# A fifth pair of units with seven block products in each layer, behind one plain unit whose down projection stands on both sides of the pair's first block

## The reference

```python
FFN_HIDDEN = 5632

def swiglu(h, w_gate, w_up, w_down):
    return (jax.nn.silu(h @ w_gate) * (h @ w_up)) @ w_down

for layer in range(2):
    h = rms_norm(x, mix_norm[layer])
    mix = ...                      # mixer of the layer
    x = x + mix
    h = rms_norm(x, ffn_norm[layer])
    x = x + swiglu(h, w_gate[layer], w_up[layer], w_down[layer])
return rms_norm(x, final_norm)
```

## Time and profile before

| | |
|---|---|
| time, median of 3 runs | 1944.07 us (1942.9 to 1945.13) |
| the profiled execution | 1944.98 us, span 1943.2 us |
| granted TensorE clock, mean | 0.997 |
| TensorE busy | 1925.4 us, 99% |
| VectorE busy | 1395.8 us, 72% |
| ScalarE busy | 924.5 us, 48% |
| DMA | 380.92 MB, mean 196 GB/s |

### The profile page before, as it was taken

The page is one execution under the profiler, slowest core; times in us unless marked ns, Lnnn a source line. Parts: engine busy times, 40 slices in busy tenths (PEclk is TensorE's granted clock), DMA queues, the critical chain, the costliest instruction groups (busy, mean ns, idle before and its releaser), DMA issues.

```text
span 1943.2 us, 21963 instructions
## 1 busy us (share of the span) xinstructions
PE 1925.4 (99%) x9268; PEld 1612.3 (83%) x9268; DVE 1395.8 (72%) x1040; ACT 924.5 (48%) x722; POOL 23.6 (1%) x85
## 2 busy tenths in 40 slices
PE   9999999999999999999999999999999999999997
PEld 7889999988888888888888887788888888888885
DVE  5656788865758868877779556756877868878754
ACT  6434434436434535545446345633544545545443
POOL 1000000000000000000000030000000000000000
PEclk9999999999999999999999999999999999999999
DMA  9555444455555654846666655464675654747751
GB/s 305 177 176 166 152 152 151 151 176 171 178 191 198 235 195 173 281 153 250 226 215 229 214 187 173 132 208 137 236 261 190 243 195 174 278 139 252 240 211 70
DMA packets 214730, 380.92 MB, mean 196 GB/s; under 512 B 5921, under 2 KB 55154, under 8 KB 214386
## 3 DMA queue, kind: packets, MB, share of 16 engines
q1 hardware_dynamic: 214560, 379.62, 57.5%
q10 hardware_dynamic: 82, 0.03, 0.0%
HBM read 377.53 MB, written 2.10 MB: 195 GB/s over the span
## 4 chain that ended last, share of the span: by engine, by line
PE 90%; DVE 8%; ACT 1%; issue 1%; DVEq 0%; POOL 0%; ACTq 0%; POOLq 0%
PE main L1576 39%; PE main L1582 20%; PE main L1518 8%; PE aux L1598 5%; PE main L1520 4%; DVE lo L976 4%; DVE raw L982 4%; PE aux L1602 3%; PE main L1598 2%; PE aux L1525 2%; PE main L1602 2%; PE aux L1687 1%; ACT hi L628 1%; PE main L1629 1%; PE main L1631 1%; PE main L1630 1%
## 5 line engine op out<-in xcount | busy, mean ns | idle before, releaser
L628 ACT CAST hi<-raw 128x2048 fp32r<-128x2048 f32 (+1 forms) x389 | 741.6, 1907 | 779.1 <-PE main L1582 494.1
L976 DVE TENSOR_TENSOR lo<-raw,hi 128x2048 fp32r<-128x2048 f32 x316 | 720.0, 2291 | 321.6 <-ACT hi L628 321.6
L1576 PE MATMUL main<-hi,act 128*128 128x512 f32 x1968 | 470.0, 391 | 0.0
L1576 PEld LDWEIGHTS main<-hi,act 128*128 128x128 f32 x1968 | 368.1, 188 | 77.5 <-issue 1.9
L1576 PE MATMUL main<-hi,mid 128*128 128x512 f32 x1664 | 397.0, 391 | 0.3 <-DVE mid L1243 0.3
L1576 PEld LDWEIGHTS main<-hi,mid 128*128 128x128 f32 x1664 | 310.8, 188 | 65.3 <-DVE mid L1243 1.0
L1582 PE MATMUL main<-lo,act 128*128 128x512 f32 x984 | 243.1, 389 | 0.0
L1518 PE MATMUL main<-act,hi 128*128 128x512 f32 x640 | 229.1, 401 | 0.0
L967 DVE TENSOR_TENSOR lo<-raw,hi 128x2048 fp32r<-128x2048 f32 x71 | 162.6, 2290 | 79.2 <-ACT hi L628 79.2
L1582 PEld LDWEIGHTS main<-lo,act 128*128 128x128 f32 x984 | 184.7, 188 | 38.3
L1582 PE MATMUL main<-lo,mid 128*128 128x512 f32 x832 | 205.5, 389 | 0.0
(11 more groups left out here) (169 smaller groups left out, 1287.9 us busy)
## 6 DMA issues: line engine op xcount, KB each, us to landing
raw<-in_ffn_w_gate SPq DMA_DIRECT2D x104, 1024.0 KB, 5.2
raw<-in_ffn_w_up SPq DMA_DIRECT2D x88, 1024.0 KB, 6.3
raw<-in_ffn_w_down SPq DMA_DIRECT2D x88, 1024.0 KB, 5.1
raw<-in_ab_w_in SPq DMA_DIRECT2D x55, 1024.0 KB, 5.1
raw<-in_ab_w_out SPq DMA_DIRECT2D x16, 1024.0 KB, 5.1
raw<-in_pool_w SPq DMA_DIRECT2D x4, 1024.0 KB, 5.5
xn<-in_x SPq DMA_DIRECT2D x4, 512.0 KB, 7.9
out<-xn SPq DMA_DIRECT2D x2, 768.0 KB, 4.2
```

The lines of the kernel that those rows point to most:

```text
L628: return nc.scalar.copy(out_, in_)
L976: V.tensor_tensor(lo[:, split_at(t), :], src, hi[:, split_at(t), :].bitcast(F32), ALU.subtract).then_inc(lo_ready, 1)
L1576: mm(o2[:, h, :], lhs[:, k0 + n, c, h * P:(h + 1) * P], w_hi, start=(first and c == 0 and n == 0), stop=False)
```

## The change

`UNITS` becomes `(3, 2, 2, 2, 2)`: the first group of a layer is one plain unit and a pair, the other four are pairs. Ten pairs in all. The class `Plain` goes, and `Group` has its pair's first unit as `a`.

The plain unit (unit 0) has 8 slots of gate and up as before. Its down projection no longer adds up with that of other units: it is four slots of its own, `early`. The order of the first group's slots is: gate and up of the plain unit (8), `ups[0]` of the pair (4, into `bank_a`; behind its second slot the hidden tile of the plain unit is turned), early 0 and 1, block 0 (6), early 2 and 3, block 1 (6), `g.x` (2), `ups[1]` (4), down of the pair (8). Early 0 goes into `bank_b`, early 1 into `bank_a`, and early 2 and 3 both into `bank_b`, one token half at a time (`early_half`), with two new semaphores: `half_used` (TensorE is done with half 0) and `half_added` (VectorE has added half 0 into `xn`). In the last group of a layer the three turnings of `xn` (layer 0) or the three products with the final gain (layer 1) stand behind down slots 4, 5 and 6 (`AFTER`).

```diff
-UNITS = (2, 2, 2, 2, 3)
+UNITS = (3, 2, 2, 2, 2)
...
+PAIR_DOWN = ((0, 0), (1, 0), (0, 1), (1, 1), (2, 0), (2, 1), (3, 0), (3, 1))
+AFTER = {4: 0, 5: 1, 6: 2}
...
+        g = Group(layer, u + n - 2, len(UNITS) * layer + index)
+        if g.first:
+            g.slot, g.job = s, j
+            up_a = s + 8
+            k0 = up_a + 4 + 2
+            k1 = k0 + BLOCK + 2
+            g.early = (up_a + 4, up_a + 5, k0 + BLOCK, k0 + BLOCK + 1)
+            j += 6
```

On VectorE (ScalarE has the same order of `prepare`, without `early_down`):

```diff
+                def up_a(g):
+
+                    for b in range(4):
+                        prepare(g.ups[0] + b + AHEAD)
+                        if g.first and b == 1:
+                            take_hidden(layer, g.a - 1, 0)
+
+                def early_down(g, m):
+
+                    xs = xn[:, :, WIDE * m:WIDE * (m + 1)]
+                    if m < 2:
+                        add_residual(Count(g.early[m]), (bank_b, bank_a)[m], m)
+                        return
+                    for h in range(2):
+                        if h == 0:
+                            ve.wait_ge(half_used, 2 * layer + m - 1)
+                        else:
+                            ve.wait_ge(slot_used, g.early[m] + 1)
+                        V.tensor_tensor(xs[:, h], xs[:, h], bank_b[:, h, :], ALU.add
+                                        ).then_inc(half_added if h == 0 else job_emptied, 1)
...
+                        up_a(g)
+                        for m in range(2):
+                            early_down(g, m)
+                            prepare(g.early[m] + AHEAD)
+                    for i in range(BLOCK):
+                        prepare(g.blocks[0] + i + AHEAD)
+                    if g.first:
+                        for m in range(2, 4):
+                            early_down(g, m)
+                            prepare(g.early[m] + AHEAD)
+                    else:
+                        up_a(g)
                     if g.blocks:
-                        for i in range(BLOCK):
-                            prepare(g.blocks[0] + i + AHEAD)
-                        for b in range(4):
-                            prepare(g.ups[0] + b + AHEAD)
                         for i in range(BLOCK):
                             prepare(g.blocks[1] + i + AHEAD)
```

On TensorE:

```diff
@@ gate_block @@
                 product(s + 2, bank_q3, sum_tiles(k, 1, 0), start, end)
+                if k == 0 and g.first:
+                    pe.wait_ge(job_emptied, g.job + 4)
                 product(s + 3, bank_q6, sum_tiles(k, 0, 0), start, end)
...
+                def up_a(g, bank_):
+
+                    for b in range(4):
+                        wide(g.ups[0] + b, bank_, act, 4 * b, b == 0, b == 3)
+                        if g.first and b == 1:
+                            pe.wait_ge(job_emptied, g.job + 2)
+                            turn_hidden(layer, g.a - 1, 1)
+
+                def early_half(s, m, h):
+
+                    if m == 3:
+                        pe.wait_ge(half_added if h == 0 else job_emptied, 2 * layer + 1 if h == 0 else g.job + 5)
+                    at = split_at(s)
+                    for n in range(4):
+                        w_hi, w_lo = (a[:, at, n * WIDE:(n + 1) * WIDE] for a in (hi, lo))
+                        t_hi, t_lo = (mid[:, n, c, h * P:(h + 1) * P] for c in range(2))
+                        mm(bank_b[:, h, :], t_hi, w_hi, start=(n == 0), stop=False)
+                        mm(bank_b[:, h, :], t_lo, w_hi, start=False, stop=False)
+                        ins = mm(bank_b[:, h, :], t_hi, w_lo, start=False, stop=(n == 3))
+                    ins.then_inc(half_used if h == 0 else slot_used, 1)
...
+                        pe.wait_ge(job_emptied, g.job + 1)
+                        up_a(g, bank_a)
+                        pe.wait_ge(turn_taken, T_HIDDEN[layer] + 1)
+                        wide(g.early[0], bank_b, mid, 0, True, True)
+                        pe.wait_ge(up_kept, g.pair + 1)
+                        wide(g.early[1], bank_a, mid, 0, True, True)
                     if g.blocks:
-                        pe.wait_ge(job_emptied, g.j_up - 1)
+                        pe.wait_ge(job_emptied, g.job + 3 if g.first else g.j_up - 1)
                         need(pe, gates_out, g.pair)
                         pe.wait_ge(a_ready, 2 * layer + 1)
                         gate_block(g, 0)
...
+                        if g.first:
+                            for m in (2, 3):
+                                s = g.early[m]
+                                pe.wait_ge(hi_ready, s + 1)
+                                pe.wait_ge(lo_ready, s + 1)
+                                early_half(s, m, 0)
+                                early_half(s, m, 1)
+                            pe.wait_ge(job_emptied, g.j_up - 1)
```

More of the change, by code:

```diff
@@ L88 @@
     layer: int
-    unit: int
-    n: int
-    pair: int = 0
+    a: int
+    pair: int
     blocks: tuple = ()
@@ L95 @@
     j_up: int = 0
-    plain: tuple = ()
+    slot: int = 0
+    job: int = 0
+    early: tuple = ()
     down: tuple = ()
@@ L122, in ffn_groups @@
     for index, n in enumerate(UNITS):
-        g = Group(layer, u, n, (len(UNITS) - 1) * layer + index - 1)
-        alone = range(n) if g.first else range(2, n)
-        if not g.first:
-            k0, up_a, k1 = s, s + BLOCK, s + BLOCK + 4
[L127 to L136, removed]
+        g = Group(layer, u + n - 2, len(UNITS) * layer + index)
[7 more added lines that the diff above has]
+        else:
+            k0, up_a, k1 = s, s + BLOCK, s + BLOCK + 4
+        g.blocks, g.x = (k0, k1), k1 + BLOCK
+        g.ups, g.j_up = (up_a, g.x + 2), j
+        s, j = g.x + 6, j + 1
+        g.down, g.j_down = tuple((s + k, m, i) for k, (m, i) in enumerate(PAIR_DOWN)), j
+        s, j, u = s + 8, j + 4, u + n
         out.append(g)
@@ L521, in gate_block @@
                 for p, (row, u) in zip(PLACES[g.blocks[k]], ((0, 0), (0, 1), (1, 1), (1, 0))):
-                    place(p, wide_rows(w_gate[layer], WIDE * (2 * k + row), WIDE * (g.unit + u)))
+                    place(p, wide_rows(w_gate[layer], WIDE * (2 * k + row), WIDE * (g.a + u)))
             def unit(w, s, u):
@@ L1408, in _ @@
                 for g in groups:
                     c21, e = sig[:, 1, :], g_of[:, 1, 1, :]
-                    u0 = 2 * (UNIT_ALL * layer + g.unit)
+                    u0 = 2 * (UNIT_ALL * layer + g.a)
+                    if g.first:
+                        for b in range(8):
+                            s = g.slot + b
+                            if b == 3:
+                                ve.wait_ge(row_rstd, norm + 1)
+                                gate_out(layer, g.a - 1, 1, norm, T_HIDDEN[layer])
+                            if b == 7:
+                                ve.wait_ge(job_emptied, g.job + 1)
+                                up_out(s, 1, norm)
+                            prepare(s + AHEAD)
+                            start_of_layer(layer, b, norm)
+                        up_a(g)
+                        for m in range(2):
+                            early_down(g, m)
+                            prepare(g.early[m] + AHEAD)
```

176 lines of the change are left out of this document (84 added, 92 removed).

## The result

The changed kernel takes 1955.38 us (median of 6 runs, 1953.91 to 1956.43), the kernel before 1943.78 beside it (6 runs, 1942.90 to 1945.13). The ratio is 1.0057, with a 95% interval of 1.0047 to 1.0068: 0.6% slower, where 1953.4 us was predicted.

A forecast was written before the change was run, and what follows sets the result against it. TensorE, busy 99% of the span, was taken to bound the kernel, so matmuls removed are time gained and waits time lost. -9.6 + 2 x 7.8 + 3.4 = +9.4 us on the median 1944.07 gave 1953.4; range 1946.5 to 1957.0.

The forecast's parts named there:

- Block 0: First pair's block 0: TensorE waits for early_down(0) and lo of products 2 and 3; 2.55 us of waits, +2.2 us.
- Early 3: Half 0 of early 3 waits for VectorE's half addition, queued behind block 1's first lo and two sums: +5.7 us a layer.
- the late and the punctual case: Load for block 1's first product: if late, early 3 waits 5.7 us; if punctual, 4.1.
- Rival (c): At half 0 of early 3, additions into xn do not hold TensorE up: 1934.5 us; chance 0.05 with its neighbours.
- The clock: Around early 3's wait the clock falls, eight to nine matmuls run at 0.427 us: 1.7 us a layer, +3.4 us.
- Block 1: First pair's block 1, behind early 3: no wait, as VectorE is ahead for once; -0.2 us a layer.
- The fifth pair and what costs nothing: Each layer's fifth pair replaces two plain units: -9.6 us for two layers; extra additions, splits, sums and turnings cost nothing.

The follow-up runs named there:

- the experiments on the order: Changed kernel with early 2's half additions on VectorE moved ahead of block 1's first preparation and between its lo and sums: 1944.82 us, ratio 1.0007 to the kernel before.
- VectorE's path: Changed kernel with one more same-size subtraction on VectorE ahead of the lo of block 1's first product in first pairs: 1960.67 us, ratio 1.0089.
- the last kernel: Changed kernel with all four early slots half by half between the first pair's blocks, early 3's addition behind block 1's fourth preparation: 1935.20 us, ratio 0.9960.
- filled wait: Changed kernel with 22 small matmuls on zeros put on TensorE in front of early 3, inside its wait: 1950.13 us, ratio 1.0032.
- short sums: Changed kernel with the two sums of block 1's first product, in first pairs, cut to 64 of 2048 columns: 1948.59 us, ratio 1.0021.
- smaller loads: Changed kernel with the loads of early 2 and 3 cut to a quarter of their bytes: 1953.49 us, ratio 1.0052.

## Why the prediction was right, step by step

Measured times of layer 0 are set on the prediction's own scale here, whose zero is the end of the last `up_a` block, 538.34 in the trace.

- **Block 0.** It starts at 11.17 (predicted 11.2), the low pass of product 2 at 18.91 (18.76) and that of product 3 at 23.32 (23.3). Early 2 starts at 30.0 (29.9). The listed waits of 0.19 and 1.37 look smaller than the 0.5 and 1.6 forecast; counted between starts the two low passes come 0.35 and 1.56 us late, and the matmuls behind each lose another 0.13. The block is 18.63 us long, 18.55 was forecast.
- **Early 3.** The load of block 1's first product has landed when its `hi` starts, at 31.69 (31.75), VectorE's first half addition starts behind the two sums at 40.25 (40.3), and early 3 starts at 41.07 (41.0). The wait is 5.33 us in layer 0 and 5.98 in layer 1 as listed, 5.48 and 6.14 between starts, as the prediction counts it (5.7). The order that makes it, `lo`, two sums, half an addition, is the one forecast, and the experiments on the order (all of the wait gone) and on VectorE's path (more work, longer wait) show it as the cause. The late load is part of it as priced: 1.6 us was the difference between the late and the punctual case, and a partly earlier load gave 1.2 us a layer. Rival (c), no wait at all, was wrong for the reason given against it; it is what the last kernel, with another order of slots and additions, comes near (1935.2 against its 1934.5).
- **The clock.** It fell in both layers. The price is 1.65 and 2.06 us where 1.7 each was chosen: seven and nine slow matmuls for eight to nine. The filled wait shows that the idle time is the cause, and 3.3 us its price by another way. The outcome was right, its footing thin, and that part is luck. The count of eight to nine was read from no row. Of the two rows that the choice was made between, the one at the kernel's start does not carry it: in the variant with all four early slots between the blocks, TensorE waits 1.97 us at the same place and the clock stays up (rows in the last section). The Trainium skill (TensorE: Matmul & The Clock Gate, HAM oscillation) has, in its example, each wait for a load followed by work at the half clock; the matmuls behind these two waits bear it out at 0.427 us each.
- **Block 1** has no wait, as forecast. Block 0 to block 1 was to take 36.95 us and took 36.99 and 38.04; layer 1 is longer by 0.65 of wait and 0.4 of clock.
- **The fifth pair and what costs nothing.** The feed-forward part went from 712.98 to 717.08 us in layer 0 (471.25 to 1188.33) and from 708.28 to 714.31 in layer 1 (1220.13 to the start of the last group of matmuls at 1934.44), +4.1 and +6.0. First pairs account for 9.5 and 10.5 more than an ordinary pair by the reckoning of the prediction (36.99 and 38.04 less 27.2, 0.3 ahead of block 0, less the 0.4 and 0.2 of an ordinary pair's blocks). That leaves -9.9 for the two fifth pairs with all small items, where -9.6 stood. Ordinary pairs still take 127.5 to 127.7 us, and the three turnings at the end of layer 0 show no wait.

The sum of +9.4 stands against +10.0 of span. The difference of the medians is 11.6 (9.1 to 13.2 by the interval of the ratio), since the profiled execution lies 1.2 us above the median of before and 0.5 below that of after. This scatter, for which the prediction had no term, is most of its miss of 2.0 us.

What stays open: where the filled wait's gain beyond the 3.3 us seen between the blocks comes from; why the clock falls behind a wait of about 2 us, at the kernel's start and elsewhere, in some of the traces and not in others; and how much of the kernel's 8.3 us could still be raised to the 10.9 us of the matmuls saved.

## What to carry to other kernels

An engine that works in program order makes a wait out of a bad place in a list: an addition into which another engine has to come back belongs ahead of preparations that nobody needs yet, but no later than the next use of the bank that it empties. Before a gain counted in matmuls is booked, write down for each new hand-over when its answer is due and what stands ahead of it, loads included. A wait of TensorE in the middle of dense work costs more than its length: those of 2.7 to 7.7 us here all cost another 1.5 to 2.1 us, nearly all of it at the lower clock, and of two near 2 us one did (1.83) and one did not (2.17).

## What the runs showed of the hardware that was not expected

- A wait of 2.73 us was enough to bring the clock down: in the kernel with the short sums early 3 lasted 7.12 us in place of 5.44. The falls at both ends of the kernel before had left open what a wait of that length does in the middle of dense work. Waits of 1.4 us inside the blocks never did. In between, in front of the second up unit, the length did not decide: 1.83 us brought the clock down (early 3's addition behind block 1's preparations, layer 1), 1.33, 1.42 and 2.17 did not.
- What the fall costs did not grow with the wait. Behind the 1.83 us it was 1.70. By the length of early 3 less 5.44 it was 1.68 and 1.73 us after waits of 2.73 and 2.90 (short sums), 1.71 and 1.61 after 4.28 and 4.55 (smaller loads), 1.65 and 2.06 after 5.33 and 5.98 (changed kernel), and 1.54 and 1.53 after 7.68 and 7.16 (VectorE's path doubled).
- Matmuls on zeros, 4.96 us of them, kept the granted clock at 1.00 (windows 576 to 584 of the filled wait) in front of a remaining wait of 0.9 us.
- At the kernel's start the length of the wait did not decide either. The clock fell there in the kernel before, in the changed kernel and in those with the doubled path and the smaller loads, and stayed up in the other seven traces. After 1.93 us of wait in the kernel before it was at 0.50 from 14 to 16; with all four early slots between the blocks it stayed up after 1.97:

```profile
11.79 0.50 PE L1659 MATMUL main<-hi,act 128*128 128x512 f32 x1 [1.97 <-DVE lo L1044]
```

```profile
14.00:16.00 2.00, 2.00 (x14) 1.77 (x13) 1.48 (x2) 1.25 (x3) 0.00 (x0) 1.00 1.05 387
```

- Stages that an edit does not touch moved by 0.5 to 2.2 us between traces: block 0 of layer 0 starts at 549.51 in the changed kernel, and at 549.00 (path doubled), 548.73 (order), 548.39 (short sums) and 547.29 (filled wait) in its first four variants, whose edits all lie behind it but for one fill of a tile on GpSimd. Differences of that size between two profiled executions should be read between two marks of each trace, not from the whole span.
